# Two transformer blocks on one core: projections, attentions, norms and gated sums of each block in one stage with an order for every engine

## The chip, the core and the metric

The kernel runs on one core of a Trainium2 chip. It uses TensorE (PE) for matmuls, VectorE (DVE) and ScalarE (ACT) for element-wise work, GpSimd (POOL) in the expert and delta stages, and SyncE (SP) to issue transfers. The metric is the device time of one execution in microseconds (us); lower is better. Three runs of the kernel before took 3628.58, 3631.92 and 3642.89 us, median 3631.92.

## The reference, cut to what matters

One sequence of 512 tokens, width 1024, float32, goes through two blocks of different kinds. Only the parts in bold are touched by the change.

First block: norm with a modulation, a gated linear recurrence, **projections with `w_in`, a differential attention, a sliding-window attention, three gated branch products and their sum**, `w_out`, then a mixture of 32 experts.

```
q = rms_norm(q, q_gain);  k = rms_norm(k, k_gain)                  # by heads of 64
s = einsum('bqhmd,bkhmd->bhmqk', q_blk, k) * DIFF_HD ** -0.5       # + bias by distance, causal
p = softmax(s);  attn = p[:, :, 0] - lam * p[:, :, 1]              # 4 heads, two maps each
o = rms_norm(einsum('bhqk,bkhe->bqhe', attn, v), subln_gain) * (1.0 - lambda_init)
...
branch_proj = einsum('bsnc,ncd->bsnd', branches, w_branch)         # 3 branches of 512
merged = einsum('bsnd,bsnd->bsd', sigmoid(gl), branch_proj);  return merged @ w_out
```

The sliding window is 128 tokens, with 8 query and 2 key heads and a sink logit. Second block: a norm, a delta rule in two directions, **three groups of 8 heads of a dilated window attention (dilation 1, 4, 16), their mixing by log-sums, two gated branch products**, `w_o`, and a gated convolutional feed-forward.

```
for gi, (window, dil) in enumerate(ATT_GROUPS):
    o_g, l_g = dilated_window_attention(q_b[:, :, gi], k_b[:, :, gi], v_b[:, :, gi], slopes[gi], dil, ...)
wts = softmax(stack(lses), axis=0);  o_b = einsum('gbsh,gbshe->bshe', wts, stack(outs))
mixed = sigmoid(gate_a) * y_a + sigmoid(gate_b) * y_b
```

## The kernel before

Everything is float32. A product with weights is done in three matmuls of 128x128 by 128x512 on operands that are split into a rounded part and a rest (`product`, lines 188 to 192): high by high, low by high, high by low. The weights come through `WeightRing`: units of 1 MB (128 partitions x 2048) are loaded by SP, ScalarE writes the rounded part (line 284), VectorE the rest (line 287), and TensorE takes the unit. In the stages of interest there are four units in the ring and two rooms for rounded parts, so a new unit is rounded when the second last one is used up. A unit holds two column groups of 128 outputs with 8 products each (24 matmuls), or four groups of a branch with 4 products each (12 matmuls).

The program is a sequence of stages. A stage has one piece of code for each engine, its own semaphores, and ends with a barrier of all engines (lines 336 to 339). Within a stage the order of each engine is the order of its code; there is no scheduler. Block 1 has, from 210 us on: `project` (4 query, 4 key groups and the values of the differential attention), `attention` (16 units: 4 heads x 4 query tiles), the norm of its output (lines 1080 to 1104), `project` again for the sliding window (6 normalised groups and the values), a transpose of the values, `attention` (8 units), `merge_branches` (6 rounds of 4 branch groups and 4 gate groups), and then `project_out`. Block 2 has, from 2549 us on, three times a stage that loads position biases, `project` (4 + 4 normalised groups and the values) and `attention` (16, 4 and 4 units), then a stage for the log-sums (lines 2500 to 2566) and `merge_branches` (4 rounds), then `project_out`.

In `project` a normalised group is squared by ScalarE, summed over heads on TensorE with a 128x128 matrix of ones (line 610), rooted by ScalarE (line 663), inverted by VectorE over 128x512 (line 695) and multiplied into the copy from PSUM (line 697). In `attention` a unit goes: scores (PE, line 888), bias and maximum (DVE, 936 and 939), exponential (ACT, 911), inverse sum and scaling (DVE, 961 to 970), transposes (PE, 867), copy (ACT, 901), product with the values (PE, 877), copy out (DVE, 923). Scores have two banks of PSUM, so up to three units are under way. In `merge_branches` ScalarE makes the sigmoid of the gate (1198), VectorE multiplies and adds (1218, 1221).

## Time and profile before

| | |
|---|---|
| profiled execution | 3635.47 us, span 3633.5 us |
| TensorE busy | 3077.8 us, 85% |
| VectorE busy | 2236.9 us, 62% |
| ScalarE busy | 1594.3 us, 44% |
| block 1, first projection to merged branches | 210.7 to 746.0 us |
| block 2, same | 2549 to 3172.3 us |
| mean granted clock | 0.898 |

The expert stage and the delta stage lie between the two regions, the feed-forward behind the second. Busy times of TensorE count overlapping matmuls once. The granted clock is TensorE's, as a share of 2.4 GHz; 0.50 is its lower level of 1.2 GHz. A float32 matmul that is not split shows as two records.

### The profile page before, as it was taken

The page shows a single profiled execution, that of the slowest core. Times are in us where ns is not written, and L with a number is a line of the kernel's source. Part 1 is how long each engine was busy: PE and PEld are TensorE (multiplying, and loading weights), DVE is VectorE, ACT ScalarE, POOL GpSimd, SP SyncE. Part 2 cuts the span into 40 slices and gives each one's busy share as a digit, 9 for nine tenths or more (in the row PEclk, how much of TensorE's full clock was granted, in tenths as well). Part 3 has the DMA queues.
Part 4 walks back from the last instruction along what each step waited for, and adds up shares of the span by engine and source line. Part 5 has one row for each costly group of instructions (what it writes and reads, how often), then busy time and mean ns, then how long its engine had stood idle before and what let it go on. Part 6 is the DMA issues. An engine that isn't in the chain of part 4 may idle for free. (4 is left out here: it accounts for less than half of the span.)

```text
span 3633.5 us, 45934 instructions
## 1 busy us (share of the span) xinstructions
PE 3077.8 (85%) x18366; PEld 2419.9 (67%) x18366; DVE 2236.9 (62%) x2035; ACT 1594.3 (44%) x1712; POOL 250.9 (7%) x149
## 2 busy tenths in 40 slices
PE   7676669976899999999999909787868778979999
PEld 3554447764787788788878707686647665767777
DVE  6555643334798999999999744465545543336643
ACT  6523232221676777777777624222232331233322
POOL 0000000002011111111111000341000000000000
PEclk9886779995999999999999959898879777989999
DMA  7320102222899999999999741000202111223322
GB/s 310 99 71 18 47 1 93 93 97 111 308 370 370 367 373 376 372 373 372 376 370 379 272 149 63 14 4 26 75 13 70 47 35 47 93 59 93 93 81 81
DMA packets 207264, 604.81 MB, mean 166 GB/s; under 512 B 11426, under 2 KB 108706, under 8 KB 170500
## 3 DMA queue, kind: packets, MB, share of 16 engines
q1 hardware_dynamic: 197744, 568.52, 42.6%
q0 software_dynamic: 9216, 33.56, 2.5%
q8 instruction: 112, 1.84, 0.2%
q10 hardware_dynamic: 148, 0.53, 0.0%
q14 instruction: 44, 0.36, 0.0%
HBM read 581.57 MB, written 21.01 MB: 166 GB/s over the span
## 5 line engine op out<-in xcount | busy, mean ns | idle before, releaser
L1743 DVE TENSOR_TENSOR weight_ring_part<-weight_ring,weight_ring_part 128x2048 fp32r<-128x2048 f32 x384 | 860.5, 2284 | 103.0 <-ACT weight_ring_part L1684 102.9
L1684 ACT ACTIVATE weight_ring_part<-weight_ring 128x2048 fp32r<-128x2048 f32 x384 | 720.1, 1914 | 254.9 <-PE ps L192 132.6
L192 PE MATMUL ps<-weight_ring_part 128*128 128x512 f32 (+1 forms) x1328 | 527.6, 397 | 0.0
L287 DVE TENSOR_TENSOR weight_ring_part<-weight_ring,weight_ring_part 128x2048 fp32r<-128x2048 f32 x135 | 307.9, 2282 | 289.9 <-ACT weight_ring_part L284 288.2
L284 ACT ACTIVATE weight_ring_part<-weight_ring 128x2048 fp32r<-128x2048 f32 x135 | 256.8, 1903 | 369.8 <-PE ps L192 147.6
L190 PE MATMUL ps<-weight_ring_part,gathered_hi 128*128 128x512 f32 x1024 | 409.6, 400 | 1.8 <-DVE gathered_lo L1752 1.8
L192 PE MATMUL ps<-weight_ring_part,gathered_hi 128*128 128x512 f32 x1024 | 406.0, 396 | 0.0
L191 PE MATMUL ps<-weight_ring_part,gathered_lo 128*128 128x512 f32 x1024 | 405.9, 396 | 0.0
L190 PE MATMUL ps<-h1T_hi,weight_ring_part 128*128 128x512 f32 (+1 forms) x776 | 317.8, 409 | 54.3 <-PEq L339 29.3
L191 PE MATMUL ps<-h1T_hi,weight_ring_part 128*128 128x512 f32 (+1 forms) x776 | 307.9, 397 | 0.0
L192 PEld LDWEIGHTS ps<-weight_ring_part 128*128 128x128 f32 (+1 forms) x1328 | 253.3, 191 | 57.1 <-issue 0.8
L190 PEld LDWEIGHTS ps<-weight_ring_part,gathered_hi 128*128 128x128 f32 x1024 | 193.0, 188 | 60.0 <-issue 7.6
L192 PEld LDWEIGHTS ps<-weight_ring_part,gathered_hi 128*128 128x128 f32 x1024 | 192.8, 188 | 47.2
L191 PEld LDWEIGHTS ps<-weight_ring_part,gathered_lo 128*128 128x128 f32 x1024 | 193.1, 189 | 45.8
L190 PEld LDWEIGHTS ps<-h1T_hi,weight_ring_part 128*128 128x128 f32 (+1 forms) x776 | 148.5, 191 | 106.0 <-issue 54.1
L190 PE MATMUL ps<-weight_ring_part,hidden_hi 128*128 128x512 f32 x512 | 204.2, 399 | 10.4 <-DVE hidden_lo L1780 6.6
L192 PE MATMUL ps<-weight_ring_part,hidden_hi 128*128 128x512 f32 x512 | 200.4, 391 | 0.0
L191 PE MATMUL ps<-weight_ring_part,hidden_lo 128*128 128x512 f32 x512 | 200.0, 391 | 0.0
L190 PE MATMUL ps<-hT_hi,weight_ring_part 128*128 128x512 f32 x376 | 155.9, 415 | 27.9 <-PEq L339 22.2
L191 PEld LDWEIGHTS ps<-h1T_hi,weight_ring_part 128*128 128x128 f32 (+1 forms) x776 | 148.3, 191 | 33.3 <-issue 3.4
L1582 POOL DMA_INDIRECT y_rows<-expert_out,y_row_of_slot x32 | 90.4, 2826 | 1017.5 <-ACT expert_out L1700 1017.5
L191 PE MATMUL ps<-hT_hi,weight_ring_part 128*128 128x512 f32 x376 | 151.3, 403 | 0.0
(450 smaller groups left out, 4774.5 us busy)
## 6 DMA issues: line engine op xcount, KB each, us to landing
weight_ring<-in_w SPq DMA_DIRECT2D x190, 2048.0 KB, 9.1
weight_ring<-in_w_in SPq DMA_DIRECT2D x58, 1024.0 KB, 5.3
weight_ring<-in_w_ada SPq DMA_DIRECT2D x24, 1024.0 KB, 14.5
weight_ring<-in_w_ffn_up SPq DMA_DIRECT2D x44, 512.0 KB, 5.1
weight_ring<-in_w_ffn_down SPq DMA_DIRECT2D x11, 1024.0 KB, 4.9
chosen_rows<-y_rows SPq DMA_DIRECT2D x4, 2048.0 KB, 13.4
weight_ring<-in_w_branch SPq DMA_DIRECT2D x6, 1024.0 KB, 5.1
x_tok<-in_x SPq DMA_DIRECT2D x2, 2048.0 KB, 13.8
```

Of the source, the lines that this page charges most:

```text
L190: nc.tensor.matmul(out, x[0], y[0], start=start, stop=False)
L191: nc.tensor.matmul(out, x[1], y[0], start=False, stop=False)
L192: return nc.tensor.matmul(out, x[0], y[1], start=False, stop=stop)
L284: self.nc.scalar.activation(hi, full, ACT.Copy).then_inc(self.rounded, 1)
L287: self.nc.vector.tensor_tensor(lo, full, hi, ALU.subtract).then_inc(self.split, 1)
L1582: nc.gpsimd.indirect_dma_start(y_rows, bass.IndirectOffsetOnAxis(y_at[:, e:e + 1], 0), y_out[:, e % 2, :], None)\
L1684: nc.scalar.activation(hi_half(h), full_half(h), ACT.Copy).then_inc(w_rounded, 1)
L1743: nc.vector.tensor_tensor(lo_half(h), full_half(h), hi_half(h), ALU.subtract).then_inc(w_split, 1)
```

## The change

Each region becomes one stage, `stream`. Its work is a list of elements (column groups of a projection or a merge), batches (norm factors), and attention units. `lay_out` runs when the program is built: it gives every step a length, a rank and what it needs, and fills three lists, one each for TensorE, ScalarE and VectorE, by taking again and again the step that can start first. `stream` then writes each engine's code in the order of its list. Waits are on the same kind of semaphores as before. A product is cut into steps of three matmuls, which stand between the steps of attention.

Further edits that go with it. Products use two banks of PSUM, scores two banks for one unit at a time, the value product one. Head sums give 128 tokens by 2 heads (`sums`), the factor of a query is multiplied in when its scores leave PSUM (`score` on VectorE, one instruction for each piece with a factor of its own), the factor of a key is spread by four matmuls (`spread`) and multiplied into the keys. Values are made like queries and transposed (`turn_v`). The gate is a tanh of half the value, and the branch is copied by ScalarE with a factor of one half. The order of the weight units follows. Position biases of block 2 are loaded in twelve pieces from within the stage. x of block 2 is stored to memory at the start of the delta stage and loaded back in `project_out`.

On TensorE in the differential attention of block 1: before, groups of transposes (L867), scores (L888) and value products (L877) follow each other.

```order
L888 MATMUL ps<-xn_tok 128x256 x2
L877 MATMUL ps<-work,x_tok 128x128 x4
L867 MATMUL ps<-const,weight_ring 128x128
L888 MATMUL ps<-xn_tok 128x384 x2
L877 MATMUL ps<-work,x_tok 128x128
L867 MATMUL ps<-const,weight_ring 128x128 x2
L888 MATMUL ps<-xn_tok 128x512 x2
L877 MATMUL ps<-work,x_tok 128x128 x2
```

In the change, within the same attention (L1248 transposes, L1259 scores, L1270 value products, L1217 head sums, L1233 sums of the output's norm, L189 to L191 products with weights):

```order
L1270 MATMUL ps<-work,x_tok 128x128
L189 MATMUL ps<-hT_hi,weight_ring_part 128x512
L190 MATMUL ps<-hT_hi,weight_ring_part 128x512
L191 MATMUL ps<-weight_ring_part 128x512
L1248 MATMUL ps<-const,weight_ring 128x128 x2
L1233 MATMUL ps<-const,weight_ring 128x1 x4
L189 MATMUL ps<-hT_hi,weight_ring_part 128x512
L190 MATMUL ps<-hT_hi,weight_ring_part 128x512
L191 MATMUL ps<-weight_ring_part 128x512
L189 MATMUL ps<-hT_hi,weight_ring_part 128x512
```

Products of later groups stand between the steps of a unit. On ScalarE at the start of that attention (L911 exponentials, L901 copies of transposed probabilities):

```order
L911 ACT_TABLE_LOAD
L911 ACTIVATE weight_ring,stats<-weight_ring,stats 128x128 x2
L911 ACTIVATE weight_ring,stats<-weight_ring,stats 128x256 x2
L901 ACTIVATE work<-ps 128x128
L911 ACTIVATE weight_ring,stats<-weight_ring,stats 128x384 x2
L901 ACTIVATE work<-ps 128x256
L911 ACTIVATE weight_ring,stats<-weight_ring,stats 128x512 x2
L901 ACTIVATE work<-ps 128x384
```

and in the change (L1398 exponentials, L1387 the same copies, L1325 squares, L1334 copies of queries, L1361 of values, L283 rounding of weights):

```order
L1398 ACT_TABLE_LOAD
L1398 ACTIVATE weight_ring,stats<-weight_ring,stats 128x128 x2
L1361 ACTIVATE x_tok<-ps 128x4x128
L1325 ACTIVATE work<-ps 128x512
L1334 ACTIVATE xn_tok<-ps 128x512
L1387 ACTIVATE work<-ps 128x128
L1398 ACTIVATE weight_ring,stats<-weight_ring,stats 128x256 x2
L1387 ACTIVATE work<-ps 128x256
L1325 ACTIVATE work<-ps 128x512
L1334 ACTIVATE xn_tok<-ps 128x512
L1398 ACTIVATE weight_ring,stats<-weight_ring,stats 128x384 x2
L283 ACTIVATE weight_ring_part<-weight_ring 128x2048
```

The exponentials of a unit now share the engine with the copies of products. On TensorE at the log-sums of block 2 (L2524 transposes, L2531 spreading of weights over heads):

```order
L867 MATMUL ps<-const,s_buf 128x128 x8
L877 MATMUL ps<-weight_ring 64x128 x8
L336 UNCONDITIONAL_BRANCH
L2519 UNCONDITIONAL_BRANCH
L2524 MATMUL ps<-const,lse 8x128 x12
L2531 MATMUL ps<-lse_t,selector 128x512 x12
L336 UNCONDITIONAL_BRANCH
```

and in the change (L1279 and L1289 are the same two; between them stand 28 steps of three products, and 118 behind):

```order
L189 MATMUL ps<-h1T_hi,weight_ring_part 128x512
L190 MATMUL ps<-h1T_hi,weight_ring_part 128x512
L191 MATMUL ps<-weight_ring_part 128x512
L1279 MATMUL ps<-const,lse 8x128 x12
L189 MATMUL ps<-h1T_hi,weight_ring_part 128x512
L190 MATMUL ps<-h1T_hi,weight_ring_part 128x512
...
L190 MATMUL ps<-h1T_hi,weight_ring_part 128x512
L191 MATMUL ps<-weight_ring_part 128x512
L1289 MATMUL ps<-late_room 128x512 x12
L189 MATMUL ps<-h1T_hi,weight_ring_part 128x512
L190 MATMUL ps<-h1T_hi,weight_ring_part 128x512
L191 MATMUL ps<-weight_ring_part 128x512
```

The two groups of the log-sums moved from a stage of their own into the products of the merge.

```diff
-            ring.add_pair(wide(w_in, 512 * j), DK, 512, by_rows=(j == 4))
+        for j in range(2):
+            ring.add_pair(wide(w_in, 512 * j), DK, 512, by_rows=False)
+        for half in range(2):
+            for j in (4, 2, 3):
+                ring.add(wide(w_in, 512 * j)[:, :, 256 * half:256 * half + 256], DK, 256)
         w_kv = a["w_kv"].rearrange("(k p) n -> p k n", p=P)
...
-                ring.add_pair(wide(w_in2, 2080 + 1536 * j + 512 * g), DK, 512, by_rows=(j == 2))
+            for half in range(2):
+                for j in (2, 0, 1):
+                    ring.add(wide(w_in2, 2080 + 1536 * j + 512 * g)[:, :, 256 * half:256 * half + 256], DK, 256)
         for w, c0 in (("w_dn_out_2", 6688), ("w_attn_out_2", 7712)):
             for j in range(2):
...
+        def lay_out(elements, batches, units, subs=(), after=(), room_after=None, out_after=None, gate_after=None, lse=False):
...
+                    job(("prod", e, k), "pe", 0.72, 9, before, *([("out", e - 2) if e >= 2 else None, ("split", x["unit"]),
+                        ("source_split", x["source"]) if x["kind"] == "branch" else None] if k == 0 else []))
+                needs = [last(e), ("out", e - 1) if e else None]
...
+            for i, u in enumerate(units):
+                one = ("evict", i - 1) if i else None
+                n, _, size = u["seg"]
+                wide = n * size / 512
+                job(("score", i), "pe", 0.2 + 0.55 * wide, 2, *[("out", e) for e in u["needs"]], keys[u["keys"] - 1], ("factors", u["batch"]), one)
+                job(("evict", i), "dve", 0.3 + 0.1 * len(u["scores"]) + 1.3 * wide + (0.8 if u.get("sinks") is not None else 0), 1, ("score", i),
+                    ("turn", i - 3) if i >= 3 else None, one)
+                job(("exp", i), "act", 0.2 + 0.3 * n + 0.55 * wide, 1, ("evict", i), ("exp", i - 1) if i else None)
+                job(("norm", i), "dve", 0.5 + 0.65 * wide, 0, ("exp", i), ("norm", i - 1) if i else None)
+                m = len(u["turns"])
+                job(("turn", i), "pe", 0.12 * m + 0.1, 1, ("norm", i), ("p_copy", i - 1) if i else None, ("turn", i - 1) if i else None)
+                job(("p_copy", i), "act", 0.2 + 0.12 * m, 0, ("turn", i), ("weigh", i - 1) if i else None)
+                job(("weigh", i), "pe", 0.12 * m + 0.1, 0, ("p_copy", i), ("read", i - 1) if i else None, ("v_copy", vs[u["v"] - 1]))
+                job(("read", i), "dve", 0.45, 0, ("weigh", i), ("read", i - 1) if i else None)
...
+            ready = {"pe": {}, "act": {}, "dve": {}}
+            free = {"pe": 0.0, "act": 0.0, "dve": 0.0}
+            orders = {"pe": [], "act": [], "dve": []}
...
+            while any(ready.values()):
+                best = None
...
+                        start = max(at, free[engine])
+                        key = (start, jobs[name][2], at, len(orders[engine]))
+                        if best is None or key < best[0]:
+                            best = (key, name, engine, start)
+                _, name, engine, start = best
+                del ready[engine][name]
+                if name[0] in spare_users:
+                    holder = (spare_users[name[0]],) + name[1:]
+                free[engine] = ended[name] = start + jobs[name][1]
+                orders[engine].append(name)
...
+        def stream(hT, elements, batches, units, order, sq, factors, v_turn, stats, s_buf, p_turned, sub=None, merge=None, side=None, lse_of=None):
...
+                    def prod(e, k):
...
+                            pe.wait_ge(source_ready, x["source"] + 1)
+                        rhs = merge["sources"][x["source"]][1:] if x["kind"] == "branch" else hT
+                        last = product(nc, ps[:, e % 2, :], cols_of(w[x["unit"]], k, P * x["part"]), [h[:, k, :] for h in rhs],
+                                       k == 0, k == steps - 1)
...
+                    def sums(b):
+                        pe.wait_ge(squared, squared_at[batches[b]["elements"][-1]])
+                        take_spare(rooted, sums_before["sums", b] + 1)
+                        for j, e in enumerate(batches[b]["elements"]):
+                            for t in range(TT):
+                                at = 8 * j + 2 * t
+                                last = nc.tensor.matmul(ps[:, 2, at:at + 2], sq[:, slot_of_square(e), elements[e]["tokens"](t)], head_sum[:, 0:P:HD],
...
+                    def spread(b, j):
+                        pe.wait_ge(factors_ready, b + 1)
+                        take_spare(keys_scaled, spread_at[b, j] + 1)
+                        wide = sq[:, slot_of_square(batches[b]["keys"][j]), :]
+                        for t in range(TT):
+                            last = nc.tensor.matmul(ps[:, 2, P * t:P * t + P], wide[:, P * t:P * t + P], ident, start=True, stop=True)
+                        last.then_inc(spread_ready, 1)
...
+                    def score(i):
+                        u = units[i]
+                        for e in u["needs"]:
+                            copied(pe, e)
+                        pe.wait_ge(keys_scaled, u["keys"])
+                        if i:
+                            pe.wait_ge(scores_read, i)
+                        for c, n, lhsT, rhs, _, _ in u["scores"]:
+                            last = nc.tensor.matmul(scores[:, c:c + n], lhsT, rhs, start=True, stop=True)
+                        last.then_inc(scores_ready, 1)
+
...
+                    for kind, *n in order["pe"]:
+                        if kind == "prod":
+                            prod(*n)
...
+                    def out(e):
...
+                        if x["kind"] == "q":
+                            nc.scalar.activation(x["dst"], bank, ACT.Copy).then_inc(bank_free[e % 2], 1)
+                        elif x["kind"] == "k":
+                            nc.scalar.activation(x["dst"], bank, ACT.Identity, scale=x["gain"], bias=0.0).then_inc(bank_free[e % 2], 1)
...
+                    def square_root(b):
+                        m = 8 * len(batches[b]["elements"])
+                        act.wait_ge(summed, sums_before["sums", b] + 1)
+                        if b >= 2:
+                            act.wait_ge(factors_ready, b - 1)
+                        nc.scalar.activation(root(b)[:, 0:m], ps[:, 2, 0:m], ACT.Sqrt, scale=1.0 / HD, bias=col("eps")).then_inc(rooted, 1)
...
+                        m = 8 * len(batches[b]["elements"])
...
+                        nc.vector.reciprocal(factor(b)[:, 0:m], root(b)[:, 0:m])
+                        dve.drain()
+                        for e in batches[b]["keys"]:
+                            at = 8 * batches[b]["elements"].index(e)
+                            nc.vector.tensor_copy(sq[:, slot_of_square(e), :].rearrange("p (n d) -> p n d", n=8),
+                                                  factor(b)[:, at:at + 8].unsqueeze(2).to_broadcast([P, 8, HD]))
+                        dve.drain().then_inc(factors_ready, 1)
...
+                    def spread(b, j):
+                        e = batches[b]["keys"][j]
+                        copied(dve, e)
+                        dve.wait_ge(spread_ready, spread_at[b, j] + 1)
+                        dst = elements[e]["dst"]
+                        nc.vector.tensor_tensor(dst, dst, ps[:, 2, :], ALU.mult).then_inc(keys_scaled, 1)
...
+                        n, pitch, size = u["seg"]
...
+                            last = nc.vector.scalar_tensor_tensor(s_row[:, c:c + m], scores[:, c:c + m], factor(u["batch"])[:, q_at:q_at + 1],
+                                                                  bias, ALU.mult, ALU.add)
+                        last.then_inc(scores_read, 1)
...
+                        at = u["at"]
...
+                    def gate(e):
...
+                        if x["source"]:
...
+                first.append(len(elements))
+                for half in range(2):
+                    elements += [dict(kind="branch", unit=unit, part=m, ends=int(m == 3), source=n) for m in range(4)]
...
+        side_room, side_part = (x[:, 8:12, :].rearrange("p s n -> p (s n)") for x in (ring.buf, ring.part))
...
+        elements = []
+        for pair in range(2):
+            for n, (kind, buf) in enumerate((("v", dv), ("q", dqT), ("k", dkT))):
+                for part in range(2):
+                    h = 2 * pair + part
+                    elements.append(dict(kind=kind, unit=3 * pair + n, part=part, ends=part, gain=gains[:, 0:1], tokens=natural,
+                                         dst=(buf[:, :, P * h:P * h + P] if kind == "v" else buf[:, h, :])))
...
+        order = lay_out(elements, batches, units, subs=[4 * h + 3 for h in range(4)], room_after=("weigh", 15), out_after=("evict", 15),
+                        gate_after=("scale", 2, 1), after=[[("evict", 15)], [("sub_mul", 3), ("score", 23)], [("read", 23)]])
+        stream(hT, elements, batches, units, order, scratch4, factors, v_turn, stats, s_buf, p_turned,
+               sub=dict(rows=[oT[:, 1, h, :] for h in range(4)], units=[4 * h + 3 for h in range(4)], wide=side_room[:, 7680:8192],
...
                 def _(sp):
-                    if load_x:
-                        sp.dma_start(x_tok[:, :, :], a["x"][0].rearrange("(t p) d -> p t d", p=P)).then_inc(x_loaded, 16)
+                    if load_x is not None:
...
+                sp.dma_start(x_mid.rearrange("(t p) d -> p t d", p=P), x_tok[:, :, :]).then_inc(x_stored, 16)
                 sp.dma_start(w_ab, w_in2[:, 2048:2080].rearrange("(k p) n -> p k n", p=P)).then_inc(ab_loaded, 16)
                 sp.dma_start(masks[:, :, :], a["joins"].rearrange("p (m i) -> p m i", i=HD)).then_inc(ab_loaded, 16)
```

## Rows read from the trace of the kernel before

**Rows 1.** Windows, block 1: length, PE, PEld, DVE, ACT, POOL busy, clock, DMA, GB/s.

```profile
210.70:288.20 77.50, 74.56 (x305) 56.63 (x304) 46.81 (x23) 24.41 (x26) 0.00 (x0) 1.00 0.21 68
288.20:375.00 86.80, 51.22 (x182) 30.51 (x182) 48.08 (x111) 28.05 (x82) 0.00 (x0) 0.58 0.02 7
...
456.20:525.00 68.80, 39.80 (x216) 30.49 (x216) 35.26 (x71) 25.23 (x82) 0.00 (x0) 0.68 0.00 0
525.00:746.00 221.00, 209.59 (x880) 164.00 (x880) 74.49 (x61) 54.41 (x47) 0.00 (x0) 0.98 0.25 81
sum 535.30, PE 431.59 PEld 321.22 DVE 253.67 ACT 153.47 POOL 0.00; mean PE 61.66 PEld 45.89 DVE 36.24 ACT 21.92 POOL 0.00
```

**Rows 2.** Windows of block 2: the three attentions, the log-sums, the sum of all eight.

```profile
2641.00:2729.50 88.50, 55.98 (x304) 34.58 (x304) 45.49 (x80) 32.28 (x82) 0.00 (x0) 0.71 0.04 13
...
2813.00:2857.00 44.00, 28.93 (x160) 25.54 (x160) 19.61 (x20) 18.48 (x70) 0.00 (x0) 0.65 0.08 25
...
2940.00:2980.00 40.00, 28.80 (x148) 25.65 (x149) 18.56 (x19) 18.32 (x70) 0.00 (x0) 0.57 0.08 27
2980.00:3026.00 46.00, 24.68 (x50) 10.07 (x48) 21.73 (x25) 7.06 (x9) 0.00 (x0) 0.55 0.00 0
...
sum 623.30, PE 506.38 PEld 391.51 DVE 293.27 ACT 187.45 POOL 0.00; mean PE 63.30 PEld 48.94 DVE 36.66 ACT 23.43 POOL 0.00
```

**Rows 3.** Windows of the merge of block 1: all its products, the first twelve.

```profile
532.30:746.00 213.70, 208.00 (x864) 162.66 (x864) 71.68 (x59) 49.96 (x44) 0.00 (x0) 0.99 0.26 84
532.30:537.30 5.00, 4.95 (x12) 3.96 (x13) 4.30 (x2) 1.18 (x1) 0.00 (x0) 0.50 0.00 0
```

**Rows 4.** Timeline of TensorE in the differential attention: start, length, what, idle before.

```profile
306.35 0.90 PE L867 MATMUL ps<-const,weight_ring 128*128 128x128 f32 x3 [3.02 <-DVE weight_ring L970]
...
310.77 1.12 PE L867 MATMUL ps<-const,weight_ring 128*128 128x128 f32 x4 [1.20 <-DVE weight_ring L970]
...
321.25 0.69 PE L867 MATMUL ps<-const,weight_ring 128*128 128x128 f32 x2 [2.72 <-DVE weight_ring L970]
```

**Rows 5.** Groups of VectorE, block 1 (three), block 2 (one): busy, mean ns, idle.

```profile
L695 DVE RECIPROCAL work<-work 128x512 f32<-128x512 f32 x8 | 26.8, 3352 | 17.9 <-ACT work L663 17.6
L695 DVE RECIPROCAL x_tok<-x_tok 128x512 f32<-128x512 f32 x6 | 20.1, 3353 | 20.6 <-ACT x_tok L663 20.5
L1102 DVE RECIPROCAL work<-work 128x512 f32<-128x512 f32 x4 | 13.4, 3347 | 4.0 <-ACT work L1095 4.0
...
L695 DVE RECIPROCAL weight_ring<-weight_ring 128x512 f32<-128x512 f32 x24 | 80.4, 3351 | 58.2 <-ACT weight_ring L663 58.2
```

**Rows 6.** Groups of small matmuls of TensorE over the span.

```profile
L1612 PE MATMUL ps<-const,gathered_rows 128*128 128x128 f32 x256 | 34.0, 277 | 5.9 <-DMA gathered_rows<-h_rows,token_of_slot 5.9
...
L877 PE MATMUL ps<-work,x_tok 128*128 128x128 f32 x80 | 21.9, 438 | 1.4 <-ACT work L901 1.3
...
L1920 PE MATMUL ps<-const,weight_ring 128*128 128x2 f32 x64 | 8.8, 259 | 0.6 <-PE ps L192 0.2
```

**Rows 7.** Timeline of ScalarE around a table load in block 1.

```profile
377.07 2.19 ACT L1092 ACTIVATE work<-branchesT 128x512 f32<-128x512 f32 x4 [3.20 <-PEq L339]
379.27 1.28 ACT L1095 ACT_TABLE_LOAD   x1
380.57 0.69 ACT L1095 ACTIVATE work<-ps,cols 128x512 f32<-128x512 f32 x1
```

**Rows 8.** Issues of DMA with us to landing; timeline of TensorE at the delta stage's start.

```profile
weight_ring<-in_w_in SPq DMA_DIRECT2D x58, 1024.0 KB, 5.3
...
x_tok<-in_x SPq DMA_DIRECT2D x2, 2048.0 KB, 13.8
...
2182.85 0.64 PE L190 MATMUL ps<-h1T_hi,weight_ring_part 128*32 128x512 f32 x1 [11.67 <-DVE weight_ring_part L2034]
```

**Rows 9.** Timeline of VectorE in the differential attention: one wide and one narrow instruction.

```profile
302.23 1.22 DVE L936 TENSOR_TENSOR weight_ring<-ps,x_tok 128x1024 f32<-128x1024 f32 x1 [2.80 <-PE ps L888]
...
315.34 0.35 DVE L970 SCALAR_TENSOR_TENSOR weight_ring<-weight_ring,stats 128x128 f32<-128x128 f32 x1
```

814 lines of the change are left out of this document (625 added, 189 removed).

## The prediction

> **What bounds the kernel now.** I read the page's first part first: TensorE is the busiest engine, at 85% of the span. Then I cut the two places that the change touches into their stages with the table of windows [rows 1, 2]. In block 1 the seven stages from the first projection to the merged branches take 535.3 us, with TensorE busy 431.6 (at mixed clocks), VectorE 253.7 and ScalarE 153.5. In block 2 the eight stages take 623.3 us, with 506.4, 293.3 and 187.5. No engine fills its region, and TensorE is the one that could. It loses time in two ways. In the attention stages it is idle 86.8 - 51.2 = 35.6, 68.8 - 39.8 = 29.0, 88.5 - 56.0 = 32.5, 44.0 - 28.9 = 15.1 and 40.0 - 28.8 = 11.2 us, together 123 us, and what it does there runs at a granted clock of 0.57 to 0.71, near the 1.2 GHz level, while in the stages of products it is 0.97 to 1.00, the 2.4 GHz level. The timeline of TensorE [rows 4] shows the idle time: each group of transposes (L867) waits 1 to 3 us for the normalised probabilities (L970). The stage works on one chain: scores, bias and maximum, exponential, sum and scaling, transpose, copy, product with the values.
>
> The second thing to see is what the merge of block 1 costs when nothing interferes: 864 product matmuls in 213.7 us, at a clock of 0.99, so 213.7 / 864 = 0.2473 us each with its waits for the next weight unit [rows 3]. At the low level twelve take 5.0 us, 0.417 each [rows 3].
>
> **The change, part by part.** The products stay: 1320 in block 1 (19 column groups of 24, and 24 + 24 groups of the merge with 12 and 24) and 1440 in block 2 (36 of 24, 16 of 12, 16 of 24). The stages go, and with them the barriers between them. What was beside nothing now lies beside products, so I sum TensorE's work at the high clock for each merged stage.
>
> Block 1. Products: 1320 x 0.2473 = 326.4 us. Attention: the same score, transpose and value matmuls; their busy time scaled by the clock that they had, 51.2 x 0.58 + 39.8 x 0.68 = 56.8 us. That the scaling holds for small matmuls is seen in transposes of the same shape: 34.0 / 256 = 0.133 us each in the expert stage, against 0.28 to 0.35 in the attention stage [rows 4, 6]. If it held for none of them, 91.0. New small matmuls: the head sums are now 128 tokens by 2 heads, 16 for four groups. The nearest row is L1920 of the same shape, 8.8 us for 32 matmuls (two records each), 0.275 [rows 6]; 14 groups x 4 x 0.275 = 15.4 us. The key factors are spread by six and the sub-norm by four groups of four 128x128 matmuls; L877 has 40 of these in 21.9 us at 0.58, so 0.32 each at full clock and 40 x 0.32 = 12.8. Sixteen 128x1 sums at 0.275 are 4.4, twenty value transposes at 0.133 are 2.7. Together 35.3; between 18 (they hide in the stream of products) and 60. Sum of TensorE: 326.4 + 56.8 + 35.3 = 418.5, plus 3 for entry and the last tail, plus stalls.
>
> Stalls. The orders put the first score behind 66 steps of three product matmuls and the last value product of attention before the 223rd of 440; in between there is nearly always a product step beside each attention step, as the piece of TensorE's order shows. So the 123 us of idle time get a filling of at least 421 steps x 0.742 = 312 us in both blocks. The filling is placed by fixed costs and can be misplaced. The costs that I can compare err on one side: four groups of head sums are planned at 1.8 us, where 16 x 0.275 is 4.4, so that TensorE comes later than planned and finds its inputs ready. I take a quarter of the 123 us, 15 us in each block; the ends are 0 and all of it. Block 1: 418.5 + 3 + 15 = 436.5 against 535.3, a gain of 98.8.
>
> Block 2. Products 1440 x 0.2473 = 356.1. Attention 56.0 x 0.71 + 28.9 x 0.65 + 28.8 x 0.57 = 75.0 (unscaled 113.7). The log-sum stage 24.7 x 0.55 = 13.6 [rows 2]. Small: 96 head sums x 0.275 = 26.4, 48 spreads x 0.32 = 15.4, 48 value transposes x 0.133 = 6.4, together 48.2. Sum 492.9, with 3 and 15 it is 510.9 against 623.3, a gain of 112.4. The log-sum chain, 46 us alone before, stands in the order with 28 product steps (20.8 us) between its transposes and its spreading, and 118 steps behind, so that the merge of the first branch covers most of it.
>
> The other engines must not become the bound. VectorE loses the wide reciprocals: 26.8 + 20.1 + 13.4 us in block 1 and 80.4 in block 2 [rows 5], and the scaling from PSUM behind each. It gains small factors, a 128x512 copy and multiply per key group (about 1.3 us each, 6 and 12 of them), and scores that are now read in 2, 4 or 8 pieces: eight of 0.35 at most are 2.8 us where one instruction took 1.2 [rows 9], in eight units of block 2. That leaves about 195 of 437 and 225 of 511 us. ScalarE gains 24 and 16 branch copies (about 0.6 each), copies of queries and keys in place of wide roots, and table loads: 27 in both regions where there were 13. A load is 1.28 us, and the next activation starts at once, 379.27 to 380.57 [rows 7]. So 14 x 1.28 = 18 us more on an engine that is idle over half of the region; I cost them at nothing beyond the stalls.
>
> The Trainium skill speaks against just this: "ScalarE: Activation LUTs", What ACT_TABLE_LOAD costs, gives about 2.66 us per switch with a drain, and asks to do all of one set before the next. By it the 14 further loads would be 37 us of ScalarE, still below its slack. The trace does not agree with the drain: no gap of 1.4 us stands on either side of the load [rows 7].
>
> The projected keys and queries of block 2 take room from x, so x is stored at the start of the delta stage and loaded again for the output projection. The store (2 MB; a load of this size landed after 13.8 us beside others) is ahead of the small weights for which TensorE already waits 11.7 us there [rows 8]. It adds between 0 and 13.8 us; I take 6, nearer to what the queue moves alone. The load is needed only behind two units of products of the last stage, about 20 us, and costs nothing. The weight units keep their ring of four; each is 5.3 us of transfer [rows 8] for 48 x 0.2473 = 11.9 us of products.
>
> **The sum.** Gain 98.8 + 112.4 - 6 = 205.2. The profiled execution took 3635.47 us (span 3633.5), 3.5 above the median of the runs: 3635.5 - 205.2 - 3.5 = 3427 us.
>
> **Rivals.**
> Chain-bound: the fixed order meets a late input at each unit, and TensorE idles as before, while products come later. For it: scores now have one bank, not two, and the value product one, so that unit i+1 waits for the eviction of unit i; ScalarE's table loads delay exponentials. Against it: the first 16 units stand in 86 steps, so TensorE's own work is (86 x 0.742 + 29.7) / 16 = 5.8 us per unit, longer than the 86.8 / 16 = 5.4 that a unit took before. Price 123 - 30 = 93 us: 3520 us.
>
> More hidden than summed: no stalls and half of the small matmuls' price: 30 + 42 less, 3355 us.
>
> Clock-bound, the slower side: waits scattered between short pieces keep TensorE at 1.2 GHz in both dense stretches. They hold 421 x 3 = 1263 products, each 0.417 - 0.247 = 0.170 dearer, 215 us; attention unscaled adds 34 + 39, the small matmuls some 50: 338 us in all, 3765 us. It makes the kernel slower than before once over 205 / 338 = 61% of these stretches run low. For it: all attention stages stand at 0.57 to 0.71. Against it: the projections of block 1 had a small matmul and a VectorE chain behind each group and kept 1.00 [rows 1].
>
> That the change does not do what it says can be left out: the orders of the three engines show it.
>
> **How the numbers follow.** Forecast (3390 to 3470) 0.62; more hidden 0.15; chain-bound 0.19; clock-bound 0.04. For 8 in 10 the range reaches into the two neighbours: 3360 to 3515. Half a per cent, 18 us, is about what a measurement of this kernel tells from no change. Slower needs the clock rival above its point: 0.03. The middle needs both a full chain rival and most unscaled work: 0.02. Faster 0.95.
>
> **What would show it.** Two stages of about 437 and 511 us in place of the groups; TensorE busy above 93% in each, with a clock above 0.95; VectorE below 50%. Wrong in the stalls: transposes waiting for VectorE over 60 us in sum. Wrong in the small matmuls: the 128x2 group not near 0.275. Wrong in the clock: a dense stretch below 0.8. The gap before the delta stage's first product should grow from 11.7 to about 18 us.

## The result and the profile after

The changed kernel takes 3452.81 us (median of 4 runs, 3449.6 to 3456.8) against 3633.45 us (the median of the three runs at the top and a fourth): ratio 0.95, 95% interval 0.9478 to 0.9523. It is 180.6 us faster; 205 were forecast (3427 us), and the range of 3360 to 3515 held the time. Run again beside the last experiments it took 3446.23 us (3441.9 to 3450.7), ratio 0.9487 (0.9471 to 0.9504). So two kernels measured at different times are told apart below only when they are more than some 7 us apart.

The windows of the changed kernel answer to [rows 1 to 3]: length, busy time of PE, PEld, DVE, ACT and POOL, granted clock, DMA share, GB/s. The first line is all of block 1's stage, the fourth all of block 2's.

```profile
207.10:629.80 422.70, 409.41 (x1980) 318.40 (x1980) 197.77 (x323) 176.41 (x302) 0.00 (x0) 0.97 0.21 67
262.00:375.00 113.00, 108.96 (x541) 81.85 (x540) 66.27 (x141) 57.36 (x116) 0.00 (x0) 0.91 0.17 52
470.00:629.80 159.80, 155.82 (x657) 121.72 (x654) 55.97 (x49) 46.27 (x49) 0.00 (x0) 1.00 0.27 86
2445.90:2983.40 537.50, 525.78 (x2452) 411.78 (x2452) 219.93 (x300) 205.73 (x379) 0.00 (x0) 0.92 0.20 62
2700.00:2900.00 200.00, 197.27 (x866) 154.30 (x867) 87.82 (x122) 77.08 (x161) 0.00 (x0) 0.89 0.18 56
2900.00:2983.40 83.40, 81.28 (x344) 63.59 (x342) 31.32 (x26) 25.23 (x26) 0.00 (x0) 1.00 0.28 89
```

Between the same points as [rows 1, 2], block 1 took 422.7 us (535.3 before, 436.5 forecast) and block 2 537.5 (623.3 before, 510.9 forecast). From their first product on they are 421.3 and 531.0 us; the experiments below are compared by this. In the windows above TensorE is busy 97 and 98% of the time, VectorE 47 and 41%; the wide reciprocals [rows 5] are gone. Yet the granted clock of block 2 is 0.92, and 0.89 in its middle, where TensorE is busy 98.6% of the time; at the end, where only the merge's products are left, it is 1.00. The loss is no longer idle time, it is products at the 1.2 GHz level.

Groups of TensorE, first in block 1's stage, then in block 2's (busy us, mean ns, idle before and its releaser):

```profile
L1248 PE MATMUL ps<-const,weight_ring 128*128 128x128 f32 x96 | 15.4, 284 | 0.9 <-DVE weight_ring L1545 0.5 <-PE ps L191 0.3
L1217 PE MATMUL ps<-const,work 128*128 128x2 f32 x112 | 14.1, 260 | 0.0
L1270 PE MATMUL ps<-work,x_tok 128*128 128x128 f32 x80 | 13.8, 310 | 1.5 <-ACT work L1387 1.5
```

```profile
L189 PE MATMUL ps<-h1T_hi,weight_ring_part 128*128 128x512 f32 x416 | 182.1, 438 | 9.3 <-PE ps L191 6.5 <-PEq L338 2.8
L1259 PE MATMUL ps<-xn_tok 64*128 64x128 f32 (+2 forms) x192 | 40.4, 455 | 0.3 <-PE ps L191 0.3
L1217 PE MATMUL ps<-const,weight_ring 128*128 128x2 f32 x192 | 33.8, 311 | 0.0
```

The transposes (L1248) that waited 1 to 3 us each for VectorE [rows 4] wait 0.9 us in all. The head sums (L1217) have two records each: 14.1 / 56 = 0.252 us in block 1, 33.8 / 96 = 0.352 in block 2. They differ by what they read. Two groups of 16, both in block 2; the first reads 128 neighbouring tokens in every sum, the second takes every fourth token in its first eight sums (the queries of dilation 4 and 16):

```profile
2550.53 3.63 PE L1217 MATMUL ps<-const,weight_ring 128*128 128x2 f32 x32
```

```profile
2801.71 0.40 PE L191 MATMUL ps<-dn_out_part,weight_ring_part 128*128 128x512 f32 x1
2801.94 5.91 PE L1217 MATMUL ps<-const,weight_ring 128*128 128x2 f32 x32
2807.71 0.77 PE L189 MATMUL ps<-x_tok_part,weight_ring_part 128*128 128x512 f32 x1
2808.28 0.63 PE L190 MATMUL ps<-x_tok_part,weight_ring_part 128*128 128x512 f32 x1
...
2813.40 0.48 PE L190 MATMUL ps<-x_tok_part,weight_ring_part 128*128 128x512 f32 x1
2813.72 0.39 PE L191 MATMUL ps<-dn_out_part,weight_ring_part 128*128 128x512 f32 x1
```

The first group ran at a granted clock of 1.00 throughout, and its records start every 0.112 us, so a sum takes 0.22. In the second the first sixteen records start every 0.233 us, also at 1.00, so a sum takes 0.47; the others start every 0.112 until the clock falls, then every 0.213. So a sum over every fourth token costs twice as much at the high level. It costs the same 0.47 at the low one: in the group at 2616.03 the clock falls at its thirteenth record, and the next strided ones keep 0.233.

The same timeline shows behind what the clock falls: the head sums above, and here 8 score matmuls of 64 rows, followed by products:

```profile
2711.22 3.37 PE L1259 MATMUL ps<-xn_tok 64*128 64x128 f32 x16
2714.52 0.75 PE L189 MATMUL ps<-h1T_hi,weight_ring_part 128*128 128x512 f32 x1
2715.06 0.63 PE L190 MATMUL ps<-h1T_hi,weight_ring_part 128*128 128x512 f32 x1
...
2718.04 0.40 PE L191 MATMUL ps<-weight_ring_part 128*128 128x512 f32 x1
```

There is no gap between these instructions. Products start every 0.23 us and last 0.40 before the narrow matmuls. Behind the head sums they start every 0.43 and last 0.63 for 5.7 us; behind the scores for 3.5 us. The granted clock falls 13 times in block 2's stage: six times in or right behind a group of head sums, six times at the end of one of the eight groups of strided scores, and once in the twelve matmuls of 8 rows that spread the log-sums (L1289). Read from start to start, 128 of the stage's 1440 product matmuls go at the low level and take 0.441 us, 1312 at the high one take 0.243.

The store of x shows where the delta stage begins. The gap before its first product was 11.67 us [rows 8], with ScalarE waiting 5.8 us for the masks at the head of that chain. Now ScalarE waits 11.8, and the product

```profile
2076.22 0.63 PE L189 MATMUL ps<-h1T_hi,weight_ring_part 128*32 128x512 f32 x1 [17.66 <-DVE weight_ring_part L2699]
```

The rest of the kernel should be as it was, but from block 2's output projection to the end it takes 466.6 us where it took 457.4 (3454.7 - 2988.1, and 3633.5 - 3176.1). TensorE's idle time there is nearly the same, 31.4 us before and 32.8 after. What differs are the means of product matmuls that nobody edited, before (first fence) and after. The rows with 1024 and 512 instructions are from the expert stage, the one with 528 from the feed-forward at the end:

```profile
L192 PE MATMUL ps<-weight_ring_part,gathered_hi 128*128 128x512 f32 x1024 | 406.0, 396 | 0.0
L192 PE MATMUL ps<-weight_ring_part,hidden_hi 128*128 128x512 f32 x512 | 200.4, 391 | 0.0
L192 PE MATMUL ps<-weight_ring_part 128*128 128x512 f32 x528 | 207.1, 392 | 0.0
```

```profile
L191 PE MATMUL ps<-weight_ring_part,gathered_hi 128*128 128x512 f32 x1024 | 399.5, 390 | 0.0
L191 PE MATMUL ps<-weight_ring_part,hidden_hi 128*128 128x512 f32 x512 | 203.2, 397 | 0.0
L191 PE MATMUL ps<-weight_ring_part 128*128 128x512 f32 x528 | 209.0, 396 | 0.0
```

### The profile page after: what moved, and what is told of

It reads as the page before. It is cut to its first block and busy times, and to the rows that moved or that the text cites. A ratio compares the mean times of both kernels' runs of the same rounds, so it can differ in the third digit from the quotient of the medians.

```text
span 3454.7 us, 46979 instructions
## 1 busy us (share of the span) xinstructions
PE 3077.4 (89%) x18858; PEld 2438.9 (71%) x18858; DVE 2108.2 (61%) x2119; ACT 1637.4 (47%) x1790; POOL 251.0 (7%) x149
## 5 line engine op out<-in xcount | busy, mean ns | idle before, releaser
L191 PE MATMUL ps<-weight_ring_part 128*128 128x512 f32 (+1 forms) x1456 | 586.2, 403 | 0.0
L189 PE MATMUL ps<-weight_ring_part,gathered_hi 128*128 128x512 f32 x1024 | 403.4, 394 | 1.7 <-DVE gathered_lo L2414 1.7
L189 PE MATMUL ps<-h1T_hi,weight_ring_part 128*128 128x512 f32 (+1 forms) x872 | 367.1, 421 | 40.1 <-DVE weight_ring_part L2699 17.7
L191 PE MATMUL ps<-weight_ring_part,gathered_hi 128*128 128x512 f32 x1024 | 399.5, 390 | 0.0
L283 ACT ACTIVATE weight_ring_part<-weight_ring 128x2048 fp32r<-128x2048 f32 x135 | 257.0, 1904 | 211.8 <-PE ps L191 116.9
L190 PE MATMUL ps<-h1T_hi,weight_ring_part 128*128 128x512 f32 (+1 forms) x872 | 354.6, 407 | 0.0
L191 PEld LDWEIGHTS ps<-weight_ring_part 128*128 128x128 f32 (+1 forms) x1456 | 281.5, 193 | 70.2 <-issue 0.8
L189 PEld LDWEIGHTS ps<-h1T_hi,weight_ring_part 128*128 128x128 f32 (+1 forms) x872 | 170.7, 196 | 104.7 <-issue 51.3
L189 PEld LDWEIGHTS ps<-weight_ring_part,gathered_hi 128*128 128x128 f32 x1024 | 192.9, 188 | 53.0 <-DVE weight_ring_part L2405 8.0
L189 PE MATMUL ps<-weight_ring_part,hidden_hi 128*128 128x512 f32 x512 | 208.3, 407 | 18.7 <-DVE weight_ring_part L2405 11.6
L191 PEld LDWEIGHTS ps<-weight_ring_part,gathered_hi 128*128 128x128 f32 x1024 | 192.8, 188 | 40.6
L191 PE MATMUL ps<-weight_ring_part,hidden_hi 128*128 128x512 f32 x512 | 203.2, 397 | 0.0
L190 PEld LDWEIGHTS ps<-h1T_hi,weight_ring_part 128*128 128x128 f32 (+1 forms) x872 | 170.8, 196 | 34.7 <-issue 0.5
L189 PE MATMUL ps<-hT_hi,weight_ring_part 128*128 128x512 f32 x408 | 172.8, 424 | 14.3 <-PEq L338 8.2
L190 PE MATMUL ps<-hT_hi,weight_ring_part 128*128 128x512 f32 x408 | 164.2, 402 | 0.0
## 6 DMA issues: line engine op xcount, KB each, us to landing
weight_ring<-in_w_ada SPq DMA_DIRECT2D x24, 1024.0 KB, 13.8
```

What stands on the lines that cost most here:

```text
L189: nc.tensor.matmul(out, x[0], y[0], start=start, stop=False)
L190: nc.tensor.matmul(out, x[1], y[0], start=False, stop=False)
L191: return nc.tensor.matmul(out, x[0], y[1], start=False, stop=stop)
L283: self.nc.scalar.activation(hi, full, ACT.Copy).then_inc(self.rounded, 1)
```

## The experiments

**Is the overlap the gain?** Two orders with the same instructions. In the first, `lay_out` gets two more needs, so that each part stands behind the one before it:

```
+   ("read", last_of[e // 12 - 1]) if e >= 12 else None      # first product of the next projections
+   (("w_sum",) if lse else ("read", N - 1)) if x["kind"] in ("branch", "gate")   # first product of the merge
+   last(rows_of[u["batch"] // 2])                           # first score: the last projection of its group
```

> The same instructions as the changed kernel, but laid out one part behind the other in both blocks: project a group, attend over it, project the next, attend, and the merge's products last of all. My theory is that the overlap is the gain, and the other edits (the tanh gate, the norm's factor folded into the scores) nearly nothing: then block 1 takes about what its parts took before, 75 + 87 + 45 + 69 + 215 = some 490 to 530 us instead of 423.5, block 2 some 590 to 620 instead of 534, and the whole comes back to about 3590 us (3560 to 3630). The rival, that fewer and shorter instructions made the gain and not the order, expects no more than 3480 us.

Measured: 3567.8 us (ratio 0.9828, 0.9805 to 0.9851). Its windows of the two stages, then groups of block 2:

```profile
210.30:685.00 474.70, 427.28 (x1980) 333.80 (x1980) 197.74 (x322) 174.49 (x300) 0.00 (x0) 0.92 0.19 59
2501.80:3094.10 592.30, 533.23 (x2436) 421.15 (x2436) 219.57 (x300) 198.00 (x371) 0.00 (x0) 0.88 0.19 56
```

```profile
L1252 PE MATMUL ps<-const,s_buf 128*128 128x128 f32 x144 | 29.6, 363 | 26.8 <-DVE s_buf L1544 25.3 <-ACT late_room L1391 1.5
L1293 PE MATMUL ps<-late_room 8*128 8x512 f32 x24 | 20.8, 1063 | 14.1 <-DVEq L1602 14.1
```

The waits are back (26.8 us before block 2's transposes, 14.1 for the weights from the log-sums), and small matmuls run low again. The order is worth 3567.8 - 3452.8 = 115.0 us, 53 in block 1 and 61 in block 2. Some 86 of these are idle time of TensorE: 47 and 59 us in the two stages, against 12 and 9 with the order of the change. The other 65.7 us against the kernel before come without this overlap. The theory held, but "nearly nothing" for the other edits was wrong: they are a third of the gain of the whole, and in the two regions, where nothing else is lost, some 84 of 198 us (535.3 + 623.3 before, 474.7 + 592.3 here and 7.9 ahead of the first products). Which of them does it was not tried; that the wide reciprocals and the barriers between parts are gone is my reading.

The second order keeps projections beside attentions and holds back the merge alone:

```
+   (("w_sum",) if lse else ("read", N - 1)) if x["kind"] in ("branch", "gate") else None
```

> Projections and attentions stay interleaved, but in both blocks the first product of the merge waits until the last attention (in block 2 the sum over the three groups) is done, so that nothing of the merge lies beside VectorE's and ScalarE's work. Theory: the projections alone do not cover the attention. Block 1 then needs some 250 us up to the merge (VectorE alone has about 185 us of work there, in chains) and 214 us for it, 464 in all, 40 more than now; block 2 bares the chain of the logs of sums (about 34 us before the change): 565, 30 more. Whole: about 3520 us (3490 to 3550). Rival 1: the projections cover everything, and the merge's place is worth nothing: 3455 to 3465. Rival 2: the merge is all of the cover: the same as in the kernel that does one part behind the other, about 3590.

Measured: 3512.93 us (0.9675, 0.9654 to 0.9695), blocks 443.2 and 564.8 us. So the 115 us split about evenly, taken away in this order: 60.1 for the merge's products beside the attention, 54.9 for the projections beside it. Neither cover does it alone.

**What does a head sum cost?** Each one is issued twice:

```
+   for again in range(2):
        last = nc.tensor.matmul(ps[:, 2, at:at + 2], sq[...], head_sum[:, 0:P:HD], start=True, stop=True)
```

> Each of the 152 head sums (128x128 by 128x2, fp32) is issued twice into the same columns; nothing else changes. By the groups of the changed kernel one costs 0.252 us in block 1 (56 of them) and 0.352 us in block 2 (96): the double costs 14 + 34 = 48 us if each has the price of the first, whole 3500. If the second of two costs only the pitch of a stream of them at full clock (0.13 us), 20 us, 3473. If a longer run of narrow matmuls also lowers the granted clock for the products behind it, more than 48: some 60 to 70, 3515 to 3525, and the mean granted clock of block 2's stage falls from 0.92 to about 0.88.

Measured: 3512.22 us (0.9666, 0.9642 to 0.969), so 59.4 us for 152 more: 0.39 each, above the 0.25 to 0.35 of the rows. The reason given for "more than 48" did not show: behind the doubled run the clock is low no longer than behind the single one, and the clock of block 2 is 0.90, not 0.88.

```profile
2717.67 14.22 PE L1218 MATMUL ps<-const,weight_ring 128*128 128x2 f32 x64
2731.76 0.77 PE L189 MATMUL ps<-h1T_hi,weight_ring_part 128*128 128x512 f32 x1
...
2734.85 0.39 PE L190 MATMUL ps<-h1T_hi,weight_ring_part 128*128 128x512 f32 x1
```

The price is in the sums themselves: from start to start they take 76.6 + 38.0 us in the two stages where they took 33.0 + 13.5, 68 us more for 152 sums, while 43 fewer products run low. In the run above the sixteen strided sums take 0.47 each as before; the sixteen others now all run low, at 0.43 instead of 0.22. The products behind are low for only 3.1 us here.

**Would shorter runs keep the clock up?** Behind each piece of 2 to 4 narrow matmuls TensorE does the next product step of its order:

```
+   def between():
+       at = next((i for i, step in enumerate(steps_left) if step[0] == "prod"), None)
+       if at is not None and steps_left[at][2]:
+           prod(*steps_left.pop(at)[1:])
```

> The narrow matmuls of both stages (head sums, spreadings, scores, transposes, weighings) are cut into pieces of 2 to 4, and behind each piece stands one step of a product (three 128x512 matmuls) that stood later in the order; every engine's instructions and waits are the same in number. In the changed kernel TensorE is busy 98% of block 2's stage and yet is granted 0.92, and the products run at half clock for 3 to 6 us behind each longer run of narrow matmuls. Theory: the clock falls because of the runs' length; cut up, it stays at 0.97 or more in block 2, whose stage shrinks from 534 to about 510 us: whole about 3430 us (3420 to 3440). Rival 1: it is the share of narrow work and not its distribution: no change, 3445 to 3460. Rival 2: each switch between wide and narrow costs some 0.1 us: with about 130 more of them 13 us slower, 3466.

Measured: 3478.93 us (0.9577, 0.9556 to 0.9599), 26 us slower than the changed kernel. Rival 2 had the sign and half of the size. Block 1 is unchanged (420.6 us), block 2 takes 552.6 at a clock of 0.91.

```profile
2747.21 1.80 PE L1225 MATMUL ps<-const,weight_ring 128*128 128x2 f32 x8
2748.87 0.48 PE L189 MATMUL ps<-h1T_hi,weight_ring_part 128*128 128x512 f32 x1
...
2749.65 1.80 PE L1225 MATMUL ps<-const,weight_ring 128*128 128x2 f32 x8
2751.30 0.78 PE L189 MATMUL ps<-h1T_hi,weight_ring_part 128*128 128x512 f32 x1
```

The first step between two pieces still runs at the high level, the next at the low one: behind strided sums the clock falls in spite of the step between them. The number of low products in block 2 stays as it was, 126 for 128. Of the 21.6 us that the stage grew, 9 are the 1314 products at the high level, which take 0.250 instead of 0.243: behind each piece the first product takes 0.31 us to the start of the next, and not 0.23. Another 10 are narrow matmuls and the log-sums' spreading, more of which meet the low level, and some 2 the low products. In block 1, whose sums read neighbouring tokens, the stage is at the low level for 14 us instead of 27, but it is no shorter: its products at the high level take 0.245 instead of 0.243, and TensorE idles for 14.3 instead of 11.9. So cutting up the narrow work is no cure; its amount and form have to change.

**Head sums in one pass.** The squares are written as fp32r (into the room of the rounded parts, not where they were), and so is a copy of the 0/1 matrix:

```
-   nc.scalar.activation(sq[:, slot_of_square(e), :], ps[:, e % 2, :], ACT.Square)
+   nc.scalar.activation(sq_r[:, slot_of_square(e), :], ps[:, e % 2, :], ACT.Square)
-   nc.tensor.matmul(ps[:, 2, at:at + 2], sq[...], head_sum[:, 0:P:HD], ...)
+   nc.tensor.matmul(ps[:, 2, at:at + 2], sq_r[...], head_r, ...)
```

> The squares and the 0/1 matrix of the 152 head sums of both blocks are kept as fp32r instead of fp32 (rounded when they are written), so each head sum is one pass instead of the several of an fp32 matmul; nothing else changes. In the changed kernel 16 head sums of block 2 take 5.75 us, and the products behind them run at the lower clock for 5.7 us more. Theory: both go. The sums shrink to a third or less (6 groups of 5.75 to 2 us: 22 us; block 1 7 to 10 us), the run gets too short for the clock to fall behind it (6 times some 2.8 us: 17 us): 45 us, whole about 3405 us (3395 to 3420). Rival 1: one pass costs as much as the fp32 matmul (the weights' load decides): 3445 to 3455. Rival 2: the sums shrink but the clock falls all the same, since it is the scores' groups that lower it: about 30 us, 3423.

Measured: 3407.86 us (0.9383, 0.9356 to 0.9409), 45 us less than the changed kernel (38 less than its second measurement), as the theory had it. Windows and groups:

```profile
210.60:615.20 404.60, 392.31 (x1924) 304.33 (x1924) 196.96 (x322) 175.88 (x302) 0.00 (x0) 1.00 0.22 70
2433.50:2930.50 497.00, 487.99 (x2340) 377.37 (x2340) 220.14 (x300) 203.28 (x375) 0.00 (x0) 0.96 0.22 67
```

```profile
L1219 PE MATMUL ps<-head_r,weight_ring_part 128*128 128x2 f32 x96 | 14.4, 280 | 0.0
L1219 PE MATMUL ps<-head_r,work_part 128*128 128x2 f32 x56 | 6.7, 248 | 0.0
```

A sum is now one record, with the same starts as before: 0.112 us behind each other, 0.233 when it takes every fourth token. The sums' busy time falls from 33.8 + 14.1 to 14.4 + 6.7 us, by 26.8. The stages shrink by 16.7 + 34.0 = 50.7. Of the difference, 24 us, the products make 21, since fewer of them run low (51 instead of 128 in block 2, 8 instead of 35 in block 1); the clock goes from 0.92 to 0.96 in block 2.

**Scores on alternating halves of the rows.**

```
-   8 * (c % 2) + 2 * t + p, here[:, p, :]) for p in range(2) for t in range(TT)],
+   8 * (c % 2) + 2 * t + p, here[:, p, :]) for t in range(TT) for p in range(2)],
```

> The eight score matmuls of a unit of the groups 1 and 2 of block 2 (64x128, K of 64 rows) are issued in pairs, one on rows 0 to 63 and one on rows 64 to 127, instead of four on one half and four on the other; nothing else changes. They take 3.30 us a unit (8 units) and the products behind them run at the lower clock for 3.5 us; four such matmuls of block 1, which alternate the halves, take 0.65 us. Theory: the alternation is the difference: 3.3 goes to about 1.4 us, and the lower clock behind them to almost nothing: 8 x (1.9 + 1.7) = 29 us, whole about 3424 us. Rival: the reads with a stride of four tokens cost it, which block 1 hasn't: no change, 3448 to 3456.

Measured: 3428.18 us (0.9436, 0.942 to 0.9453), 18.0 us less than the unchanged kernel run beside it. The same group in its timeline:

```profile
2694.98 2.25 PE L1259 MATMUL ps<-xn_tok 64*128 64x128 f32 x16
2697.16 0.50 PE L189 MATMUL ps<-h1T_hi,weight_ring_part 128*128 128x512 f32 x1
2697.50 0.39 PE L190 MATMUL ps<-h1T_hi,weight_ring_part 128*128 128x512 f32 x1
```

3.30 us became 2.18 (1.4 was expected), and the granted clock stays at 1.00 behind it; in the whole stage it falls at no group of scores any more, only at the entry, at head sums and at the log-sums. One matmul still lasts 422 ns in the mean, as before; two on different halves lie over each other. The group of block 1 that was the model, 0.65 us for four, is still 1.7 times as quick per matmul. The likely cause is the stride: here pairs of records start every 0.236 us, which is the price of a record over every fourth token in the head sums (0.233), and there every 0.112, the price over neighbouring ones. No run took the stride away from the scores.

**The addresses.** The change allots `key_gain`, 4 bytes in a partition, ahead of nearly all other tiles, which moves them by 32 bytes. First the kernel before, with such a tile and nothing else:

```
+   unused = sb(ctx, "unused", [P, 1])
```

> The kernel before with one unused tile of 4 bytes per partition where the change has key_gain, nothing else. If the address does it, the means of the product matmuls become those of the changed kernel in the stages that the change didn't touch: gathered_hi 400 to 394 ns, hidden_hi 399 to 407, the last matrices' 392 to 396, the FFN's stretch 387.5 to about 396 us, and the whole moves up by 5 to 20 us, to some 3645. If the address has nothing to do with it, all of these stay as they were and the whole is within 5 us of the kernel before.

Measured: 3643.76 us, 10.4 more than the kernel before (12 and 17 runs; ratio 1.0033, 1.0019 to 1.0046). Its groups take the values of the changed kernel:

```profile
L192 PE MATMUL ps<-weight_ring_part,gathered_hi 128*128 128x512 f32 x1024 | 400.3, 391 | 0.0
L192 PE MATMUL ps<-weight_ring_part,hidden_hi 128*128 128x512 f32 x512 | 203.1, 397 | 0.0
L192 PE MATMUL ps<-weight_ring_part 128*128 128x512 f32 x528 | 209.0, 396 | 0.0
```

The stretch at the end took 465.6 us against 457.4; each stretch from the first block on ahead of it took what it took before within 1 us. Then the changed kernel with the old addresses modulo 512:

```
-   key_gain = sb(ctx, "key_gain", [P, 1])
+   key_gain = sb(ctx, "key_gain", [P, 128])
```

> The changed kernel with key_gain allotted 512 bytes instead of 4 (one column used), so that all tiles behind it keep the address they had in the kernel before, modulo 512. Theory (the unused 4-byte tile made the kernel before 10.4 us slower): some 10 us come back, whole about 3442 us, and the means go back to those of before: hidden_hi 399 and 391 ns, the last matrices 392, the FFN's stretch about 388 us; gathered_hi goes back too, from 394 to 400. Rival: in the changed kernel other things (the order, the ring's writes) set these means: whole 3450 or more, means as they are.

Measured: 3429.89 us (0.945, 0.9433 to 0.9468), 16.3 less than the unchanged kernel beside it. In the two profiles 7.2 us of this lie in the end stretch (459.4 instead of 466.6) and 11.0 in block 2's stage, where the products at the high level take 0.241 instead of 0.243 us (4 us) and 90 instead of 126 run low (7 us). The second part need not be the addresses: that stage also took 525.3 us instead of 530.5 in the run with the later store below, whose code for it is unchanged. hidden_hi reads

```profile
L191 PE MATMUL ps<-weight_ring_part,hidden_hi 128*128 128x512 f32 x512 | 200.1, 391 | 0.0
```

The unchanged kernel beside it:

> The changed kernel once more, unchanged, on the same chip as the three kernels beside it: both theories of the addresses and of the store expect its median within 5 us of 3452.8, so that gains of 6 to 10 us can be told from a drift of one chip. If it comes out at 3444, the gains measured for the aligned tiles and for the later store were drift.

3446.23 us, so between "same" and "drift"; the kernels measured beside it (this one, the alternating scores and all four together) are held against this value. My first rule for the addresses, multiples of 64 bytes, is not the right one:

```
+   if 0 < nc.sbuf_base % 64 <= 32:
+       stack.enter_context(nc.sbuf_tensor(f"pad_{nc.sbuf_base}_{len(PADS)}", [P, 32 // 4], F32))
```

> The changed kernel with one unused piece of 32 bytes ahead of every tile that would begin at 32 bytes past a multiple of 64: all tiles of all stages begin at multiples of 64 bytes in a partition; instructions, orders and waits are the same. Why: the change puts a tile of 4 bytes (key_gain) ahead of nearly all others, and with it h1T_hi, hidden_hi and ffn_hidden moved from a multiple of 64 bytes to 32 past one, while gathered_hi moved the other way. In the traces the mean of a product matmul went from 399 to 407 ns (first one of hidden_hi), 392 to 396 (the 528 of the last matrices), and from 400 to 394 for gathered_hi. Theory: the address is the cause of the 8 us that the FFN at the end takes more (395.7 against 387.5 us) with the same instructions and waits, and of about as much in the other stages: FFN back to about 388, blocks 3 to 5 us shorter each, hidden_hi back to 399, gathered_hi still 394; whole about 3433 us (3425 to 3442). Rival: these means drift from one program to another for another reason: 3448 to 3457, means unchanged.

3443.49 us (0.9468, 0.9446 to 0.9491): half of the expected gain at best, not to be told from drift. The 528 of the feed-forward went back to 391 ns, but gathered_hi went back to 400 ns too, although it begins at a multiple of 64 as in the changed kernel, where it had 394. That addresses set the pitch is shown; which property of them does is open.

**The store of x.**

```
-   sp.dma_start(x_mid..., x_tok[:, :, :])          # ahead of w_ab and masks
+   sp.dma_start(x_mid..., x_tok[:, :, :])          # behind them
```

> The store of x to device memory (x_mid, 2 MB) is issued behind the two loads of the delta stage's first instructions (w_ab and the masks) instead of ahead of them. The changed kernel's ScalarE waits 11.8 us for them there, the kernel before 5.8: theory: 6 us come back, the wait is 5.8 again, whole 3447 us. Rival: the same bytes then delay the weights behind it: the wait goes to 5.8, but TensorE waits as much more for the first unit of weights: 3450 to 3456.

3443.66 us (0.947, 0.9449 to 0.9491). The wait fell from 11.8 to 6.6 us:

```profile
L2654 ACT ACTIVATE weight_ring_part<-weight_ring 128x256 fp32r<-128x256 f32 x1 | 0.4, 416 | 6.6 <-DMA masks<-in_joins 6.6
```

The gap before the first product of the delta stage fell with it, from 17.66 to 12.42 us, so the rival (the weights come later instead) is out. The stretch between the blocks took 1800 us, against 1811 and 1802 in the two profiles of the changed kernel. The shorter wait is shown, the whole gain (3 to 9 us) is within the drift.

**All four together** (fp32r sums, alternating scores, old addresses, later store):

> The changed kernel with the head sums in fp32r, the store of x behind the two small loads, the alternating scores and the addresses of the kernel before together. If the four add up: 45 for the sums, 9 for the store, 10 for the addresses and 0 to 29 for the scores: 3389 us without and 3360 us with the last. If part of each gain is the same lower clock counted twice, some 3395 to 3405.

3374.18 us (3372.7 to 3377.1, 5 runs; ratio 0.929, 0.9276 to 0.9304): 258 us below the kernel before and 72 below the changed one. One by one the gains are 38 to 45, 18, 16.3 and about 6, together 78 to 85, so nearly all of it adds up; the forecast with the scores at their full 29 us was 3360. Its two stages:

```profile
211.60:617.50 405.90, 393.54 (x1924) 305.75 (x1924) 196.98 (x322) 175.81 (x302) 0.00 (x0) 0.99 0.22 69
2427.40:2906.70 479.30, 470.25 (x2340) 365.27 (x2340) 219.91 (x300) 203.20 (x375) 0.00 (x0) 0.97 0.23 70
```

## Why the prediction was right, and where its terms were off

The mechanism was right: work on TensorE's path decides, VectorE and ScalarE fit beside it, and the order fills the idle time. The two orders of the first experiments show that the overlap is real and is the larger part.

Where the terms are summed from start to start, the stages of the change are made up as follows (us, measured and, in brackets, forecast; gaps under 0.15 us are left out).

| | block 1 | block 2 |
|---|---|---|
| products with their own waits at a weight unit's end | 336.3 (326.4) | 384.6 (356.1) |
| attention and other narrow matmuls | 81.0 (92.1) | 129.5 (123.2) |
| log-sums | none | 17.0 (13.6) |
| entry, and waits for other engines | 5.0 (18) | 6.5 (18) |
| stage | 422.7 (436.5) | 537.5 (510.9) |

**Stalls and entry** (15 + 3 us in each block). All waits of TensorE with the entry are 13.3 and 15.4 us, which looks like the 18 and 18 forecast, and is so by luck. Most of it is TensorE's own turn at a weight unit's end (PE ps in the groups, 7.9 and 8.9 us), and that wait was already in the price of 0.2473. The stalls that the term meant, for a late input from another engine, were 3.6 us in block 1 and none that shows in block 2. The filling hid nearly everything.

**Small matmuls and attention, block 1** (56.8 + 35.3 = 92.1). From start to start they took 81.0 us. The scaling of old busy times by the clock held on the safe side (transposes of block 1 start every 0.109 us at the high level and every 0.213 at the low one), and the 128x2 group cost 0.252 instead of 0.275.

**Products, block 2** (1440 x 0.2473 = 356.1). This is the mis-sized term: they took 384.6 with their own waits, 0.267 each, and make up more than the whole of the 26.6 us that block 2 is over. The price of 0.2473 came from a merge with nothing between its products [rows 3], where twelve ran at the low level; here 128 ran at 0.441, which is 25 us more than at the 0.243 of the others. The forecast asked for a clock above 0.95 and got 0.92. It took a low clock to be a matter of idle time, as the stages of before suggested, and priced it only as a rival for the dense stretches as a whole. The runs show that it follows narrow work without any idle time: halving the records of the head sums gave back 21 us in products besides 27 in the sums, and alternating the scores ended the falls behind them.

**Head sums, block 2** (96 x 0.275 = 26.4): 33.0 us from start to start, and 0.352 each in the rows, which the prediction had named as a sign of being wrong. The row that the price came from reads neighbouring tokens, and 32 of these 96 sums take every fourth. At the high level all the time they would be 64 x 0.224 + 32 x 0.467 = 29.3 us; the rest is the low clock.

**The store of x** (6 us): the gap grew from 11.67 to 17.66 us. Right.

**What was in no term.** The four-byte tile: 10.4 us in the kernel before, up to 16.3 in the changed one. The sum counted instructions and waits, and this changes how long the same instructions take. The stretch between the blocks was 11 us longer than before in the first profile and 3 in the second; the gap of the store is there in both (17.7 and 17.8 us), and what moved the rest of the stretch is not known.

So the profiled execution gained 113 + 86 us in the blocks (98.8 + 112.4 forecast), and lost 9 at the end and 11 between the blocks (6 forecast). That the whole came out within 26 us is in part luck too: block 1 was 13.8 under its forecast, block 2 26.6 over. **Rivals:** chain-bound did not happen in either stage. Clock-bound happened on a small scale and by another cause: 9% of block 2's products ran low, not 61%, and TensorE did not wait before they did. **Table loads** cost nothing visible: ScalarE is busy 42 and 38% of the stages, and the only waits of TensorE for it are 1.7 us in block 1.

## What to carry to other kernels

When idle time has been filled, price TensorE by its forms: a run of fp32 matmuls of two columns, or of matmuls on one half of the rows, costs its own time and then again in the products behind it. Ask of each small matmul whether it reads with a stride; here that alone doubled a head sum. Save those matmuls (one pass in fp32r, halves in alternation) rather than spreading them out. When a term comes out right, look whether it is made of what you meant. And after any change look at groups that nobody edited: if their mean moved by 1 to 2%, compare the tiles' addresses before looking for a cause in the order.
